# Gated delta net: rates with tokens in partitions, and the two heads of a pair half a level apart in the triangular inverse

## What is computed

```python
h = rmsnorm(x, norm_mix_g[0]) * (1 + scale) + shift
proj = h @ w_in                      # q, k, v, gate of 8 heads of 128, and a_in, b_in: 8 columns each
q, k, v = silu(causal_depthwise_conv(...)); q = l2norm(q) * 128 ** -0.5; k = l2norm(k)
beta = sigmoid(b_in)
g = -exp(a_log) * softplus(a_in + dt_bias)         # one rate for each token and head
# per head, in chunks: g_cum = cumsum(g); decay = exp(g_cum_i - g_cum_j), lower triangle
# L = strict lower triangle of (k * beta) k^T * decay;  A = L + I
# u = A^-1 (v * beta);  w = A^-1 (k * beta * exp(g_cum));  attn = (q k^T) * decay
# per chunk: v_new = u - w S;  o = (q exp(g_cum)) S + attn v_new;  S = S g_last + (k exp(..))^T v_new
o = rmsnorm(o, norm_g) * silu(gate);  y = o @ w_out
```

## Time and profile before

| | |
|---|---|
| runs | 2624.57, 2624.92, 2629.37 us; median 2624.92 |
| the profiled execution | 2623.83 us, its span 2622.0 us |
| TensorE, matmuls | busy 2410.0 us (92%), 12144 instructions |
| TensorE, weight loads | busy 1890.2 us (72%), beside the matmuls |
| VectorE / ScalarE / GpSimd | busy 1123.8 us (43%) / 903.0 us (34%) / 357.3 us (14%) |
| mean granted clock of TensorE | 0.958 of full speed |
| DMA | 259.80 MB, mean 99 GB/s |
| chain that ended last | TensorE 73% |

### The profile page before, as it was taken

One profiled execution on the slowest core, in us unless ns is written; L12 is line 12 of the kernel. 1 busy time (PEld: TensorE's weight loads), 2 busy tenths in 40 slices (PEclk: granted clock), 3 DMA queues, 4 the chain that ended last, 5 costly groups with the idle time before them and its releaser, 6 DMA issues.

```text
span 2622.0 us, 30221 instructions
## 1 busy us (share of the span) xinstructions
PE 2410.0 (92%) x12144; PEld 1890.2 (72%) x12144; DVE 1123.8 (43%) x1186; ACT 903.0 (34%) x1086; POOL 357.3 (14%) x164
## 2 busy tenths in 40 slices
PE   7899999989999978889999998999987798999997
PEld 4577877768888755567888886777765586788886
DVE  3757654552332455444332235342256524433234
ACT  4445553432312344433232224333233422422122
POOL 0246574357600000000000000000000000000000
PEclk9899999989999988899999999999998799999999
DMA  6233432335422313222222223111210022222222
GB/s 268 82 129 121 153 121 85 124 129 178 175 86 90 112 60 117 80 80 81 96 86 100 87 96 117 65 64 64 96 48 32 30 83 80 81 96 96 96 80 96
DMA packets 38435, 259.80 MB, mean 99 GB/s; under 512 B 4280, under 2 KB 4536, under 8 KB 8144
## 3 DMA queue, kind: packets, MB, share of 16 engines
q1 hardware_dynamic: 38352, 258.59, 27.0%
HBM read 256.42 MB, written 2.15 MB: 99 GB/s over the span
## 4 chain that ended last, share of the span: by engine, by line
PE 73%; issue 9%; POOL 8%; DVE 5%; ACT 3%; DMA 1%; SPq 0%; POOLq 0%; DVEq 0%; ACTq 0%
PE D L268 18%; PE D L269 18%; PE D L270 18%; POOL adar L325 4%; POOL adar L323 3%; PE D L283 3%; PE D L284 3%; PE D L285 3%; DMA fw<-in_ada 1%; PE D L1527 1%; PE D L304 1%; PE D L305 1%; PE D L303 1%; ACT hi L312 1%; PE D L1543 1%
## 5 line engine op out<-in xcount | busy, mean ns | idle before, releaser
L316 DVE TENSOR_TENSOR lo<-raw,hi 128x2048 fp32r<-128x2048 f32 (+1 forms) x185 | 423.8, 2291 | 460.7 <-ACT hi L312 460.5
L268 PE MATMUL D<-hH,lo 128*128 128x512 f32 x1456 | 585.5, 402 | 0.0
L269 PE MATMUL D<-hL,hi 128*128 128x512 f32 x1456 | 575.3, 395 | 0.0
L270 PE MATMUL D<-hH,hi 128*128 128x512 f32 x1456 | 575.0, 395 | 0.0
L312 ACT ACTIVATE hi<-raw 128x2048 fp32r<-128x2048 f32 (+1 forms) x185 | 342.9, 1853 | 498.5 <-PE D L270 285.3
L268 PEld LDWEIGHTS D<-hH,lo 128*128 128x128 f32 x1456 | 274.9, 189 | 70.6 <-issue 8.0
L269 PEld LDWEIGHTS D<-hL,hi 128*128 128x128 f32 x1456 | 275.0, 189 | 66.7 <-issue 4.0
L270 PEld LDWEIGHTS D<-hH,hi 128*128 128x128 f32 x1456 | 274.5, 189 | 65.2
L325 POOL TENSOR_TENSOR adar<-adar 128x1024 f32<-128x1024 f32 (+2 forms) x120 | 201.8, 1682 | 9.4
L323 POOL TENSOR_TENSOR adar<-adar,cact 128x2048 f32<-128x2048 f32 x40 | 155.6, 3889 | 347.5 <-DMA adar<-in_ada 237.6
L269 PE MATMUL D<-aL,hi 128*128 128x512 f32 x444 | 176.0, 396 | 0.0
(11 more groups left out here) (379 smaller groups left out, 3435.3 us busy)
## 6 DMA issues: line engine op xcount, KB each, us to landing
raw<-in_slabs SPq DMA_DIRECT2D x185, 1024.0 KB, 4.8
adar<-in_ada SPq DMA_DIRECT2D x42, 1024.0 KB, 4.8
fw<-in_ada SPq DMA_DIRECT2D x6, 1024.0 KB, 20.6
x<-in_xin SPq DMA_DIRECT2D x1, 2048.0 KB, 10.4
dt<-bcast SPq DMA_DIRECT2D x8, 256.0 KB, 3.5
dtb<-bcast SPq DMA_DIRECT2D x8, 256.0 KB, 4.4
qd<-bcast SPq DMA_DIRECT2D x8, 256.0 KB, 7.3
out<-x SPq DMA_DIRECT2D x1, 2048.0 KB, 6.3
```

The costliest lines, as they stand in the source:

```text
L268: T_.matmul(o, lo[s.slot][:, w], H[:, k, :], start=(k == 0), stop=False)
L269: T_.matmul(o, hi[s.slot][:, w], L[:, k, :], start=False, stop=False)
L270: last = T_.matmul(o, hi[s.slot][:, w], H[:, k, :], start=False, stop=(k == kc - 1))
L316: V_.tensor_tensor(lo[s.slot][:, 0:n], raw[s.slot][:, 0:n], hi[s.slot][:, 0:n], ALU.subtract).then_inc(lo_ready, 1)
```

## The change

Part one, the rates. The product takes the tokens of `hH`/`hL` as weights and the 16 rate columns of slab 0 as the moving operand (`rates_pe`): its results are 128x16 for each of four chunks, in four banks, so that all following instructions are on 128 partitions x 32 elements (`tk`). The bias and the factor of each head are brought to all partitions by a small matmul at the very start (`heads_dve`, `heads_pe`). The running sum is a matmul with a triangle of ones (`rates_pe_2`). `tsc` comes directly; only for the broadcasts are three transposes made (`rows_pe`) and written to DRAM. `fill(44)`, `fill(4)` becomes 8, 4, 16, 4, 6, 5, 5 around these parts and the square sums. ScalarE and VectorE treat the second half of the first keys after the logarithms of q. Part two, the levels: the second product of head 1 moves behind the first product of head 0 of the next level. Part three: the output norm's second matmul with ones moves between the Gram products of the next pair. The diff, cut to its core:

```diff
+        tk = go[:, 0, :].rearrange("p (a t h) -> p a t h", t=NT, h=GH)
+        tri = go[:, 1, 0:P]
+        rowb = go[0:NT * GH, 2, 0:3 * P]
+        diag, hcol = small[0:GH, 16:32], small[:, 32:48]
+        bcast = nc.dram_tensor("bcast", (3 * NT * GH, P), fp32, kind="Internal").ap()
...
+        def rates_pe(pe, ready):
+            s = Slab(G_AB)
+            pe.wait_ge(lo_ready, s.plus(1))
+            pe.wait_ge(rms_ready, 1)
+            cols = lambda t_, k: t_[s.slot].rearrange("p (k j n) -> p k j n", k=KC, j=2)[:, k, :, 0:GH]
+            for k in range(KC):
+                ready(k)
+                for t in range(NT):
+                    tok = slice(t * P, t * P + P)
+                    T_.matmul(AB_BANK[t], hL[:, k, tok], cols(hi, k), start=(k == 0), stop=False)
+                    T_.matmul(AB_BANK[t], hH[:, k, tok], cols(lo, k), start=False, stop=False)
+                    last = T_.matmul(AB_BANK[t], hH[:, k, tok], cols(hi, k), start=False, stop=(k == KC - 1))
+            last.then_inc(slab_done, 1)
...
+        def rates_dve_1(dve, chain):
             L = chain.link
-            a_, u_ = rtmp[:, 0, :], rtmp[:, 1, :]
-            beta = rows[:, 1, :]
             dve.wait_ge(slab_done, 1)
-            L(V_.tensor_scalar(a_, D[0][0:GH, 0, :], vec[0:GH, V["dt_b"]:V["dt_b"] + 1], None, ALU.add))
-            L(V_.tensor_copy(beta, D[0][0:GH, 1, :]))
-            V_.scalar_tensor_tensor(out=u_, in0=a_, scalar=-1.0, in1=a_, op0=ALU.mult, op1=ALU.max).then_inc(bank_free[0], 1)
-        def rows_dve_2(dve, chain):
+            V_.tensor_scalar(tri, neg, -1.0, None, ALU.is_ge)
+            for t in range(NT):
+                V_.tensor_tensor(a_[:, t], AB_BANK[t][:, 0:GH], hcol[:, 0:GH], ALU.add)
+                last = V_.tensor_copy(b_[:, t], AB_BANK[t][:, GH:2 * GH])
+            last.then_inc(bank_free[0], 1)
+            dve.wait_ge(bank_free[0], 1)
+            V_.scalar_tensor_tensor(out=u_, in0=a_, scalar=-1.0, in1=a_, op0=ALU.mult, op1=ALU.max).then_inc(gg["rowd"], 1)
...
+        def rates_pe_2(pe):
+            pe.wait_ge(gg["rowd"], 3)
+            T_.matmul(W[:, 0:NT * GH], tri, g_.rearrange("p t h -> p (t h)"), start=True, stop=True)
+            T_.matmul(W[:, NT * GH:2 * NT * GH], ones, g_.rearrange("p t h -> p (t h)"), start=True,
+                      stop=True).then_inc(gg["rowp"], 1)
+        def rates_dve_3(dve):
             dve.wait_ge(gg["rowp"], 1)
-            V_.tensor_copy(tsc[:].rearrange("p a t h -> p (a t h)"), W[:, 0:4 * NT * GH]).then_inc(gg["tsc"], 1)
-            dve.wait_ge(gg["tsc"], 1)
+            V_.tensor_copy(tsc[:, 0].rearrange("p t h -> p (t h)"), W[:, 0:NT * GH]).then_inc(gg["rowd"], 1)
+            dve.wait_ge(gg["rowd"], 4)
+            V_.tensor_tensor(df_.rearrange("p t h -> p (t h)"), W[:, NT * GH:2 * NT * GH],
+                             tsc[:, 0].rearrange("p t h -> p (t h)"), ALU.subtract).then_inc(gg["rowd"], 1)
+            dve.wait_ge(gg["row"], 6)
+            V_.scalar_tensor_tensor(out=tsc[:, 3], in0=tsc[:, 1], scalar=-1.0, in1=eg_, op0=ALU.mult,
+                                    op1=ALU.mult).then_inc(gg["tsc"], 1)
...
         def rows_pe(pe):
-            pe.wait_ge(gg["rowd"], 3)
+            pe.wait_ge(gg["row"], 5)
+            pe.wait_ge(gg["rowd"], 5)
+            for a, src in enumerate((tsc[:, 0], tsc[:, 1], eg_)):
+                last = T_.transpose(W[0:NT * GH, a * P:a * P + P], src.rearrange("p t h -> p (t h)"), ident)
             last.then_inc(gg["rowp"], 1)
+        def rows_dve(dve):
+            dve.wait_ge(gg["rowp"], 2)
+            V_.tensor_copy(rowb, W[0:NT * GH, 0:3 * P]).then_inc(gg["tsc"], 1)
+        def rates_act(act):
+            act.wait_ge(gg["rowd"], 1)
+            S_.preload_act_table_set("natural_log_exp_and_others")
+            S_.activation(u_, u_, ACT.Exp, scale=-1.0).then_inc(gg["row"], 1)
+            act.wait_ge(gg["rowd"], 2)
+            S_.activation(ln_, w_, ACT.Ln).then_inc(gg["row"], 1)
+            act.wait_ge(gg["rowd"], 4)
+            S_.activation(eg_, tsc[:, 0], ACT.Exp).then_inc(gg["row"], 1)
+            S_.activation(tsc[:, 1], b_, ACT.Sigmoid).then_inc(gg["row"], 1)
+            act.wait_ge(gg["rowd"], 5)
+            S_.activation(tsc[:, 2], df_, ACT.Exp).then_inc(gg["row"], 1)
         def rows_out(sp):
...
+            sp.wait_ge(gg["tsc"], 2)
+            for a in range(3):
+                sp.dma_start(bcast[a * NT * GH:(a + 1) * NT * GH, :],
+                             rowb[:, a * P:a * P + P]).then_inc(gg["row_out"], 16)
...
+            rates_act(act)
             for m in range(2):
                 silu(qs[0], 1, m)
             for m in range(2):
                 square_unit(qs[0], fs, m, m + 1)
             split_hi(act, Slab(3))
-            nle()
-            w("rowd", 2)
-            S_.activation(w_, gc, ACT.Exp).then_inc(gg["row"], 1)
-            S_.activation(dl, u_, ACT.Exp).then_inc(gg["row"], 1)
-            for m in range(2):
-                silu(ks, 2, m)
-            for m in range(2):
-                square_unit(ks, xi, m, m + 3)
-            split_hi(act, Slab(4))
+            silu(ks, 2, 0)
+            square_unit(ks, xi, 0, 3)
             nle()
             for m in range(2):
                 log_unit(fs, m, m + 1)
             exp_pair(fs, 2)
             decay(0)
+            split_hi(act, Slab(4))
+            silu(ks, 2, 1)
+            square_unit(ks, xi, 1, 4)
+            nle()
             for m in range(2):
                 log_unit(xi, m, m + 3)
             exp_pair(xi, 4)
...
+            rates_dve_1(dve, chain)
+            rates_dve_2(dve, chain)
             split_lo(dve, Slab(2))
-            rows_dve_2(dve, chain)
+            rates_dve_3(dve)
+            rows_dve(dve)
             for m in range(2):
                 conv(qs[0], 0, 0, 1, m)
             split_lo(dve, Slab(3))
-            rows_dve_3(dve, chain)
-            rows_dve_4(dve)
-            for m in range(2):
-                conv(ks, 1, 0, 2, m)
-            tsc_dve(dve)
+            conv(ks, 1, 0, 2, 0)
+            gaps(0)
+            q_norm(0)
             split_lo(dve, Slab(4))
-            gaps(0)
+            conv(ks, 1, 0, 2, 1)
+            beta_decay(0)
             conv(vs, 2, 0, 3, 0)
-            q_norm(0)
-            beta_decay(0)
             k_norm(0)
...
-            fill(44)
+            fill(8)
+            rates_pe_2(pe)
+            fill(4)
             rows_pe(pe)
+            fill(16)
+            w("tsc", 2)
+            sum_squares(fs, 0, 1)
             fill(4)
-            w("tsc", 1)
-            sum_squares(fs, 0, 1)
             w("fln", 1)
             sum_squares(fs, 1, 2)
+            fill(6)
             w("fln", 2)
             sum_squares(xi, 0, 3)
+            fill(5)
             w("fln", 3)
             sum_squares(xi, 1, 4)
+            fill(5)
...
                 for m in range(2):
+                    if m and p:
+                        w("oln", 2 * p - 1)
+                        T_.matmul(W, ones, up[:, 1, :], start=True, stop=True).then_inc(gg["oss"], 1)
                     for b in heads[m]:
                         last = T_.matmul(blk(D[0], b), blk(ks, b), blk(ks, b), start=True, stop=True)
                     last.then_inc(gg["gram"], 1)
...
+                def first_product(lv, m):
+                    if lv == 1:
+                        w("xi", 2 * p + m + 1)
+                    else:
+                        w("xx", 14 * p + 2 * (lv - 1) + m + 1)
+                    level_product(lv, m, D[0], up, xi).then_inc(gg["pp"], 1)
+                    if lv > 1:
+                        turn(lv - 1, m, D[2])
+                def second_product(lv, m):
+                    w("pb", 12 * p + 2 * (lv - 1) + m + 1)
+                    if lv == 1:
+                        w("att", p + 1)
+                    else:
+                        w("zz", 12 * p + 2 * (lv - 2) + m + 1)
+                    level_product(lv, m, D[2], zi, pb).then_inc(gg["qq"], 1)
                 for lv in range(1, 7):
-                    for m in range(2):
-                        if lv == 1:
-                            w("xi", 2 * p + m + 1)
-                        else:
-                            w("xx", 14 * p + 2 * (lv - 1) + m + 1)
-                        level_product(lv, m, D[0], up, xi).then_inc(gg["pp"], 1)
-                        if lv > 1:
-                            turn(lv - 1, m, D[2])
+                    first_product(lv, 0)
+                    if lv > 1:
+                        second_product(lv - 1, 1)
                     if lv in (2, 3):
                         m = lv - 2
                         w("act", 6 * p + 5 + m)
...
-                    fill(lv_fill)
-                    for m in range(2):
-                        w("pb", 12 * p + 2 * (lv - 1) + m + 1)
-                        if lv == 1:
-                            w("att", p + 1)
-                        else:
```

(51 more changed lines are left out.)

73 lines of the change are left out of this document (19 added, 54 removed).

## The result

The changed kernel takes 2678.32 us (median of four runs, 2675.27 to 2681.76), the kernel before, run beside it, 2627.14 (2624.57 to 2630.99): a ratio of 1.0194, with a 95% interval from 1.0175 to 1.0213, so about 51 us slower. The profiled execution took 2675.27 us, its span is 2673.5 us, 51.5 more than before. The forecast was 2658 with a range of 2634 to 2678; the time lies 0.3 us above its upper end. The direction was right, the size was not.

What follows compares the result with a forecast made beforehand. Pairs bound by TensorE's instruction order, the start by a chain through VectorE and ScalarE. Start -6, pairs +13.4, +19.6, +3.2, root -2.4, clock +6 sum to +33.8 us on 2623.8: 2658, range 2634 to 2678.

Steps and rivals of the forecast that it cites:

- Half a level apart: Level order in the pairs: new TensorE waits cost +13.4 us in pair 0, +19.6 in pairs 1 and 2, +3.2 in pair 3.
- the start: Stretch ahead of the pairs, 55 to 110 us: -6 us in all, from -11 to 0, Gram's 1.4 us included.
- The kdT waits: Level 2 of the pairs: TensorE waits 2.0 us for turned keys behind VectorE's copy for head 1.
- the bank's in level 4: Pair 0, level 4: the second step waits 3.7 us for the bank that a q convolution frees.
- rival 3: Only the necessary waits, no clock term or pile-up, start -11: +14 us, 2638; chance 0.15.
- Product of the rates: Start: 96 thin matmuls replace 48 wide ones and end at 53.5 instead of 54.75 us, 1.2 us gained.
- rival 4: Thin matmuls keep the clock low (22.7 us), first fills at half speed, splits contended: +50 us, 2674; chance 0.15.
- The rates behind it: Start behind the rates' product: chain with two TensorE stalls, 4.6 and 4.7 us, Gram product at T+49.7 = 103.2.
- T: Forecast end of the thin rates' product in the start, taken as 53.5 us.
- Pair 1: Second pair of heads: half-level waits for turned keys, values, convolution and split, +9.8 us.
- a term of its own: Clock in the pairs: about seven added stalls of 2 us or more lower it, +6 us, bounds 0 and +15.
- The root: Output norm's second root, moved between Gram halves: 2.4 of 5.9 us of waiting for ScalarE won.

Runs made afterwards that it cites:

- the levels alone: Kernel before with only the new half-level order of the levels: 2673.37 us, ratio 1.0169.
- Both runs with one half alone: Changed kernel with the old level order back, 2632.94 us; kernel before with the new level order alone, 2673.37 us.
- the fitted run: Changed kernel, TensorE's order untouched, VectorE's order fitted to it with other work between the two copies of a level: 2643.32 us, ratio 1.0062.
- wide product brought back: Changed kernel with the old 48 wide matmuls for the rates plus eight transposes, new rates on 128 partitions kept: 2666.72 us, ratio 1.0151.
- the run with the later turns: Changed kernel with TensorE's turns of v and their waits moved behind the second filler of levels 2 and 3: 2661.45 us, ratio 1.0121.
- the best kernel: Changed kernel with wide product and old level order back, plus a reordered start on VectorE, ScalarE and TensorE's fills: 2611.38 us, ratio 0.9942.
- root alone: Kernel before with only the output norm's second matmul with ones moved between the next Gram products: 2627.69 us, ratio 1.0011.
- levels back: Changed kernel with the old order of the levels, new rates and moved root kept: 2632.94 us, ratio 1.0014.
- wide product and levels back: Changed kernel with the old wide rates product and old level order, new rates and moved root kept: 2624.31 us, ratio 0.9995.
- the fitted kernel: Reordered start, wide product, half level with VectorE's order fitted: 2627.01 us, ratio 0.9988; fitted once more: 2630.73 us, ratio 1.0014.

## Why the prediction came out as it did

**Half a level apart: right.** Pair 2 was put at +9.8 us, measured +10.4; pair 3 at +3.2, measured +4.4. Pair 0 was put at +13.4 and came to +13.2, which is closer than the reasoning deserves: the Gram product at full speed, 1.8 us gained (1.78 us from its start to the next row's, for 3.57), lies in this stretch, while the forecast had booked its 1.4 us under the start. With the levels alone, Gram product slow as before, pair 0 lost 15.0 (84.9 for 69.8). The kdT waits, 2.0 predicted, were 2.09 us, four times; vT 4.4 predicted, 4.50 measured; the square sum's 1.4 was 1.40; GpSimd's in pair 0 5.86 for 6.7; the bank's in level 4 3.52 for 3.7. Both runs with one half alone put the same mechanism apart from the rest, and the fitted run shows its cause, VectorE's order, for 35 of the 45 us. Of rival 3 (only the necessary waits) nothing is left.

**Product of the rates: the step that failed.** "I take 53.5, 1.2 us gained": it ended at 62.04. The nearest row was the adaLN product, four one-column matmuls in the midst of wide ones at the upper clock level; it shows the price of a load at that level and nothing of what 96 of them in a row do to the level. I had the right case as rival 4, at 0.236 us each from the half-speed passes, 22.7 us, for 20.5 measured, and gave it 0.15 with the argument that adaLN products don't lower the clock. A few of them among hundreds of wide ones can't show that. That rival 4's total, 2674, lies near the measured time is in part luck: its third term, splits slowed by GpSimd, did not grow (above 2.28 us each they cost 7 us from 110 to 560 us, for 12 before). The miss is 8.5 us there and 2.0 in the first fills (7.6 us for 5.6), together 10.5 of the 17.7 us by which the growth of the span, 51.5, is above the sum, 33.8. The wide product brought back moved the Gram product by 8.3 us, 0.9 of it because TensorE also began the product sooner in that run; the 11.6 us of the whole kernel hold 4.1 us of pair 1 besides. Two small slips in the working move nothing: 96 x 0.11 is 10.6 and not 10.8, and with 0.236 for the first 4.4 us the end is 54.4 and not 54.7.

The Trainium skill, "TensorE: Matmul & The Clock Gate", section "What's actually happening", says that the gate "doesn't count instructions" and that how many matmuls run at the lower level depends on their spacing alone. The rows speak against it for these matmuls: they stand back to back from 41.54 to 62.04, and the clock is 0.50 to the last one.

**The rates behind it: right, and no gain.** From T on the chain was put at T + 49.7 us for the Gram product: T = 62.04 with 2.0 us of slower fills would give 113.7, measured 115.29. The two stalls of 4.6 and 4.7 us were 4.55 and 3.69. The two more table loads took 1.28 us each. With the 2.0 us for the clock the forecast had the Gram product at 105.2; it came 10.1 us later, and product and first fills are 10.5 of that. The 2.66 us that the Trainium skill, "ScalarE: Activation LUTs", section "What ACT_TABLE_LOAD costs", gives for a switch is not seen here: the load of 70.71 us is followed by its activation at 72.01.

**Pair 1: too small by 7 us.** The stretch to the end of its levels lost 17.1 us for 9.8. Some of it is the clock, for which the forecast had a term of its own (granted clock 0.93 from 213 to 310 us, 0.98 before). Another part had no term. VectorE's three products for the decay fell into GpSimd's multiplication, by time in the changed kernel:

```profile
214.22 4.70 DVE L996 TENSOR_TENSOR dt<-dt,tsc 128x512 f32<-128x512 f32 x2
218.96 3.27 DVE L998 TENSOR_TENSOR dt<-dt,cst 128x1024 f32<-128x1024 f32 x1
...
214.40 3.98 POOL L326 TENSOR_TENSOR adar<-adar,cact 128x2048 f32<-128x2048 f32 x1 [6.80 <-DMA adar<-in_ada]
218.46 5.71 POOL L328 TENSOR_TENSOR adar<-adar 128x1024 f32<-128x1024 f32 x3
```

and in the kernel before, where they stand in GpSimd's wait for its load and the last of them begins 0.08 us ahead of its multiplication:

```profile
193.68 1.29 DVE L963 TENSOR_TENSOR dt<-dt,tsc 128x512 f32<-128x512 f32 x2
195.00 1.23 DVE L965 TENSOR_TENSOR dt<-dt,cst 128x1024 f32<-128x1024 f32 x1
...
195.08 4.62 POOL L323 TENSOR_TENSOR adar<-adar,cact 128x2048 f32<-128x2048 f32 x1 [2.07 <-DMA adar<-in_ada]
```

That is 7.97 us for 2.52, and TensorE's waits for the value convolutions (the row of 6.7 us above), which stand around this work in VectorE's queue, were 4.0 us before. No run tried this by itself, but the traces differ in it by chance and can be laid side by side. With the half level and VectorE's old order, pair 1 takes 106.1 us where the three products take 2.52 us (the wide product brought back), and 110.2 to 113.9 in the four kernels where they take 8 to 9 (the run with the later turns, 105.6 at 8.9, has other waits and is left aside). With the old levels it takes 93.2 (before) and 91.8 (the best kernel) at 2.5 us, 95.1 (root alone) at 5.8, and 97.9 (levels back) and 98.4 (wide product and levels back) at 9.1 and 8.0. So about 4 to 5 of the 17.1 us go with this collision, and they appear without the half level too. That VectorE is slowed by 5 us or more where GpSimd's multiplication has begun ahead of one of its products, and GpSimd by 1.0 us (4.62 us for 3.60) where VectorE's last product is ahead, is what the rows show. The Trainium skill, "SBUF — State Buffer", section "SBUF: two separate sides", states an exclusive lock for a port that both engines share, which goes to whichever instruction starts first; the rows agree with it.

**The root: wrong, small.** The wait fell by 2.3 us for the 2.4 forecast, and no time was won.

**The sum.** The clock in the pairs stood at +6 us, with the root together +3.6. With the Gram product's 1.4 us counted where it lies, the start was put at -4.6 and came to +5.3, 9.9 us more; the pairs are above their own terms by 1.2, 7.3, 0.6 and 1.2 us, and the rest by 1.1, together 11.4. Less the 3.6 that makes the 17.7. How the 11.4 divide between clock, collision and root is open. The forecast should also have been 2659: 33.8 us on the median of 2624.9 are 2658.7.

## What to carry to other kernels

When an engine's order is staggered, stagger the orders of the engines that serve it in the same change: here 35 of 45 us came from leaving VectorE's two copies of a level together. And look first whether there is anything to win: in the old order TensorE had hardly waited at those places, and the fitted kernel won nothing. Price a run of thin matmuls at the clock level that it will itself bring about, not at that of isolated ones among wide work; TensorE's busy share did not tell it here (100% at 0.99 and at 0.50). At a start bound by a chain over several engines, first order the chain (the Gram product 11.4 us earlier here, with the same instructions): that was worth more than making its links cheaper (2.3 us, with the wide product). And when a stage gets longer than its forecast waits explain, look whether two engines' instructions now fall together that used to miss each other by a tenth of a us.

## What the hardware showed that was not expected

TensorE at 100% busy with 128x16 matmuls fell from a granted clock of 0.99 to 0.50 behind 24 wide and 40 thin ones, and the pitch went from 0.11 to 0.21 us. One 128x512 matmul behind every three thin ones left it at 0.50. Three VectorE products of two operands each took 3.2 times as long (7.97 for 2.52 us) where GpSimd's multiplication and sums ran beside them. Which engine pays went by who began first: in the run with levels back GpSimd's multiplication began 0.06 us ahead (198.66 and 198.72) and took 3.61 us, VectorE's first two products 6.89 for 1.29; with the wide product brought back VectorE's third product and GpSimd's multiplication both began at 206.34 and took 1.23 and 4.68 us.
